# Transposes of the activation halves one group sooner, and a second group of seven products in the first down pairs

## The reference, cut to what matters

```python
h = h + (g_attn * y_attn + g_ssm * y_ssm) @ w_out[layer]
u = rms_norm(h, mlp_norm_w[layer]) @ w_up[layer]      # 2048 -> 8192
h = h + jnp.square(jax.nn.relu(u)) @ w_down[layer]    # 8192 -> 2048
```

## Time and profile before

| | |
|---|---|
| median of 3 runs | 1985.65 us (1985.53 to 1986.33) |
| profiled execution, its own time | 1987.6 us |
| its span | 1985.6 us |
| TensorE busy | 1971.4 us, 9007 matmuls |
| VectorE, ScalarE, GpSimd busy | 1487.8, 1241.7, 175.3 us |
| granted clock of TensorE, mean | 0.999 |

### The profile page before, as it was taken

One profiled execution on the slowest core, in us unless ns is written; L12 is line 12 of the kernel. 1 busy time (PEld: TensorE's weight loads), 2 busy tenths in 40 slices (PEclk: granted clock), 3 DMA queues, 4 the chain that ended last, 5 costly groups with the idle time before them and its releaser, 6 DMA issues.

```text
span 1985.6 us, 25599 instructions
## 1 busy us (share of the span) xinstructions
PE 1971.4 (99%) x9007; PEld 1628.3 (82%) x9007; DVE 1487.8 (75%) x1769; ACT 1241.7 (63%) x1427; POOL 175.3 (9%) x179
## 2 busy tenths in 40 slices
PE   9999999999999999999999999999999999999999
PEld 8888888888887888888888888888788888878877
DVE  5777777777788766677675566577798799788878
ACT  6666666767776555555774444558657755865773
POOL 2110120112232221110000000000000000000000
PEclk9999999999999999999999999999999999999999
DMA  7777887889997666666896766767767766866865
GB/s 249 207 206 201 216 205 203 216 228 247 240 225 226 198 193 192 199 191 190 224 242 193 215 200 237 212 212 217 204 220 223 207 196 207 219 209 192 233 190 170
DMA packets 332193, 419.52 MB, mean 211 GB/s; under 512 B 147248, under 2 KB 147696, under 8 KB 331840
## 3 DMA queue, kind: packets, MB, share of 16 engines
q1 hardware_dynamic: 331184, 415.23, 73.3%
q10 hardware_dynamic: 448, 2.24, 0.3%
q0 software_dynamic: 464, 0.77, 0.2%
HBM read 382.46 MB, written 2.16 MB: 194 GB/s over the span
## 4 chain that ended last, share of the span: by engine, by line
PE 85%; DVE 6%; ACT 5%; issue 2%; DMA 2%; ACTq 0%; POOL 0%; DVEq 0%; SPq 0%; POOLq 0%
PE ps L807 20%; PE ps L809 20%; PE ps L808 20%; PE ps L1104 7%; PE ps L1105 7%; PE ps L1109 7%; DVE wlo L2413 2%; ACT f_st L1777 2%; DMA f_half<-r_half 2%; ACT whi L1712 1%; DVE t_lo__92 L2424 1%; PE ps L986 1%; PE ps L755 1%; ACT ust L1740 1%; DVE wlo L2418 1%
## 5 line engine op out<-in xcount | busy, mean ns | idle before, releaser
L1848 DVE TENSOR_TENSOR wlo<-raw,whi 128x1024 fp32r<-128x1024 f32 x450 | 569.5, 1272 | 328.3 <-ACT whi L1229 326.8
L1229 ACT ACTIVATE whi<-raw 128x1024 fp32r<-128x1024 f32 x450 | 473.2, 1057 | 323.2 <-PE ps L809 312.4
L807 PE MATMUL ps<-whi,xT_hi 128*128 128x512 f32 x1268 | 498.3, 393 | 0.0
L809 PE MATMUL ps<-whi,xT_lo 128*128 128x512 f32 x1268 | 493.8, 389 | 0.0
L808 PE MATMUL ps<-wlo,xT_hi 128*128 128x512 f32 x1268 | 493.6, 389 | 0.0
L809 PEld LDWEIGHTS ps<-whi,xT_lo 128*128 128x128 f32 x1268 | 238.0, 188 | 50.2
L807 PEld LDWEIGHTS ps<-whi,xT_hi 128*128 128x128 f32 x1268 | 238.1, 188 | 48.7 <-issue 1.4
L808 PEld LDWEIGHTS ps<-wlo,xT_hi 128*128 128x128 f32 x1268 | 238.2, 188 | 47.5
L2413 DVE TENSOR_TENSOR wlo<-raw,whi 128x1024 fp32r<-128x1024 f32 x186 | 219.5, 1219 | 41.8 <-ACT whi L1712 41.8
L1712 ACT ACTIVATE whi<-raw 128x1024 fp32r<-128x1024 f32 x187 | 192.5, 1053 | 92.8 <-PE ps L1109 92.7
L1104 PE MATMUL ps<-whi,fT_hi 128*128 128x512 f32 x416 | 163.6, 393 | 6.9 <-DVE fT_lo L2521 5.8
(11 more groups left out here) (358 smaller groups left out, 2871.8 us busy)
## 6 DMA issues: line engine op xcount, KB each, us to landing
raw<-in_w_in SPq DMA_DIRECT2D x319, 512.0 KB, 4.3
raw<-in_w_up SPq DMA_DIRECT2D x128, 512.0 KB, 4.3
raw<-in_w_down SPq DMA_DIRECT2D x128, 512.0 KB, 4.6
raw<-in_w_ssm_out SPq DMA_DIRECT2D x64, 512.0 KB, 4.3
raw<-in_w_attn_out SPq DMA_DIRECT2D x32, 512.0 KB, 4.1
raw<-in_w_out SPq DMA_DIRECT2D x32, 512.0 KB, 4.2
arow<-arows SPq DMA_DIRECT2D x16, 512.0 KB, 4.9
x_in<-in_x SPq DMA_DIRECT2D x4, 512.0 KB, 8.3
```

The costliest lines, as they stand in the source:

```text
L807: mm(dst, xh, whi[sl][:, kk, :], start=(s == 0 and kk == 0), stop=False)
L809: last = mm(dst, xl, whi[sl][:, kk, :], start=False, stop=(s == US - 1 and kk == UK - 1))
L1229: A(whi[s % SLOTS][:, :, :], raw[s % SLOTS][:, :, :], ACT.Copy).then_inc(hi_ready, 1)
L1848: V.tensor_tensor(wlo[s % SLOTS][:, :, :], raw[s % SLOTS][:, :, :], fp(whi[s % SLOTS][:, :, :]), ALU.subtract).then_inc(lo_ready, 1)
```

## The change

It adds group 5 to the groups of seven in pairs 2, 6, 10 and 14 (37 in all), and places the work that belongs to it. Form 2 is summed ahead of the low weights of group 4 instead of behind them; form 1 is rounded behind group 2's turn instead of group 4's, and form 2 behind group 3's; their low parts both come behind group 3's turn; the bank sums of those pairs move from group 5 to group 6. And in all pairs that have transposes of activation halves, SP issues these behind the loads of groups 4 and 5 instead of 5 and 6.

```diff
-DOWN_SEVEN_FIRST = (0,)
+DOWN_SEVEN_FIRST = (0, 5)
...
-SUMS_AT = (6, 5, 5, 6)
+SUMS_AT = (6, 5, 6, 6)
 SUMS_LATE = ((1, 6), (2, 3))
 JOIN_FIRST = (2, 3)
-MADE_FIRST = ()
+MADE_FIRST = ((2, 3),)
 FORMS_MADE = ((1, 4), (2, 1), (2, 3))
-FORMS_HI = ((1, 5), (2, 4), (2, 5))
-FORMS_LO = ((1, 6), (2, 5), (2, 6))
+FORMS_HI = ((1, 5), (2, 2), (2, 3))
+FORMS_LO = ((1, 6), (2, 3), (2, 3))
...
-            TURN_AT = (5, 6)
+            TURN_AT = (4, 5)
```

## The result

The changed kernel takes **1989.15 us** (median of 17 runs, 1987.97 to 1990.70); the kernel before, run in turn with it on the same chip, takes 1985.52 us (17 runs, 1984.33 to 1987.67). The ratio is 1.0018, 95% interval 1.0011 to 1.0026: 3.6 us slower, where 0.3 us faster was forecast. The time lies inside the range given, on the slow side.

What follows compares the result with a forecast made beforehand. TensorE, busy for 99% of the span, was taken as the bound. Four pairs at +0.75 us, less 2.2 and 1.6, plus 0.5, gave -0.3 us: 1985.65 to 1985.3 us, range 1980.5 to 1990.3.

Steps and rivals of the forecast that it cites:

- join of the first half: Pair 2, ScalarE: joining the transposed planes begins at 1396.50 instead of 1399.06.
- wait at group 5: Pair 2, TensorE: a new wait of 1.4 us for group 5's rounded weights, where there was none.
- wait at group 6: Pair 2, TensorE: group 6 waits 0.5 us for the second half's low part.
- wait at the next pair: Behind pair 2, TensorE waits 1.3 us on the first output bank, going on at 1430.0 instead of 1429.25.
- the transposes land late: First half's transposes land 0.8 to 1.3 us late, moving the whole chain: 1988.6 to 1990.5 us; chance 0.20.
- The clock falls at the new waits: Rival: 1.4 us of waiting is enough to lower the clock, 6.4 us more: 1991.7 us; chance 0.04.
- The work is hidden after all: Rival: group 5's weights are ready at 1408.4, new waits shrink by 1.4 a pair: 1979.7 us; chance 0.20.
- The four pairs: Sum over pairs 2, 6, 10, 14: 4 x 0.75 - 2.2 - 1.6 + 0.5 = -0.3 us, carried to the median.
- The low clock's 1.6 us: Pair 10, behind its long wait at group 4: a loss of some 1.6 us that the change would remove.
- The 2.2 us: What pairs 6, 10 and 14 wait more than pair 2 goes away: 2.2 us saved.
- The +0.5: Pair 10 shows no present wait at the next pair to set off, so 0.5 us is added.
- the runs don't hold pair 10's loss: Rival: runs without a profile lack pair 10's long wait, so 3.1 us less is saved: 1988.4 us; chance 0.08.

Runs made afterwards that it cites:

- the second profile: The kernel before, unchanged, profiled again: 1985.80 us (11 runs), ratio 1.0000, profiled execution 1985.09.
- the third: The kernel before, unchanged, profiled once more: a single execution of 1985.94 us.
- the 1989.39 and 1989.67 executions: Two single profiled executions of the changed kernel, unedited, taking 1989.39 and 1989.67 us.
- the first kernel: The kernel before with only the transposes moved behind the loads of groups 4 and 5, no further group of seven: 1977.44 us, ratio 0.9956.
- the kernel with the weight sums first: The changed kernel with group 5's weight sums made ahead of the join's low part and group 4's low weights: 1988.45 us, ratio 1.0011.
- the kernel with the second group of seven alone: The changed kernel with the transposes back behind the loads of groups 5 and 6: 2001.18 us, ratio 1.0073.
- form 2 behind: The changed kernel with form 2 summed behind group 4's low weights and group 5's weight sums again: 1985.33 us, ratio 0.9998.
- the three kernels of 1977 us: The kernel before with transposes moved everywhere (1977.44 us), only in down pairs (1977.63), or everywhere with a second group of seven at group 3 (1977.82).

## Why the prediction was wrong

**The steps inside the pair were right.** The last column is worked out start to start at 0.227 us, in pair 2.

| step | forecast | measured |
|---|---|---|
| join of the first half | 1396.50 | 1396.53 |
| end of the high part | 1400.16 | 1400.18 |
| weight sums of group 5 start | 1404.54 | 1404.56 |
| weights of group 5 rounded | 1409.76 | 1409.79 |
| wait at group 5 | 1.4 | 1.38 (the others 1.50, 1.72, 1.40) |
| wait at group 6 | 0.5 | 0.35, and 0.11 behind its first matmul |
| bank sums of `h` start | some 1428.7 | 1428.79 |
| wait at the next pair | 1.3 | 1.00, and 0.27 in the matmuls around it |
| matmuls | 8995 | 8995 |

The landings came at the low end, as I had taken them: 3.0 to 3.1 us after issue in pair 2 and 3.1 to 4.4 in the other three, where 5.2 to 8.1 stood before with the loads in front. The rival "the transposes land late" is out as the cause of the 3.6 us; late landings show in one place of the four profiles, with 0.6 us. "The clock falls at the new waits" is out too: behind 1.4 to 1.7 us of waiting the granted clock stays at 1.00 in all four pairs. "The work is hidden after all" fell by the serial chain, as was said against it.

The Trainium skill, Advanced Engine Details and Errata, section X-Bar Transpose (TRN2), has transposes as fast as regular DMAs. No run here tests that: with no load shortly in front they landed after 3.0 to 4.4 us and a load of 512 KB has a median of 4.6, but a plane of 128 x 1024 two-byte elements is half of such a load. What this case shows is what the place in the queue is worth: behind two loads they took up to 8.1. The prediction bounded them by neighbouring rows and was right to.

**The step that failed is "The four pairs", and in it the transfer to the median:** 4 x 0.75 − 2.2 − 1.6 + 0.5 = −0.3, "with the same difference" taken to 1985.65. The 3.0 is there. The terms set off against it were a property of one execution:

- The low clock's 1.6 us: absent in both further profiles of the kernel before. It was also read a little small: of the nine matmuls of the earlier trace rows, eight run from start to start in 3.52 us instead of 1.82, a loss of 1.7.
- The 2.2 us that pairs 6, 10 and 14 waited more than pair 2's 1.04 each: 0.7 and 1.4 in the further two (the sums 4.8 and 5.5 less 4 x 1.04).
- The +0.5 for pair 10's missing wait at the next pair: the two further profiles have that wait in all four pairs (0.5 us each, start to start), so there is nothing to add.

Put into the same sum, the second profile gives 3.0 − 0.7 = +2.3 and the third 3.0 − 1.4 = +1.6; the medians say +3.6. In the traces, from the MLP's first matmul to its last, the changed kernel takes 686.3, 686.6, 686.8 and 687.5 us in its four profiles, and the kernel before 686.0, 683.4 and 684.3. So the first pair of profiles is 0.2 us apart there, and the first profile of the changed kernel lies 2.9 and 2.0 above the two undisturbed ones of the kernel before. That is 0.4 to 0.6 more than the sum gives, and group 5's waits in pairs 6 and 10 (1.50 and 1.72 against pair 2's 1.38) account for it. On average the four lie 3.0 us above the two in the MLP, and 3.3 us in the whole time (1988.8 and 1985.5), which is nearly the difference of the medians.

What is left is that the first profile of the changed kernel was the fastest of its 17 executions, 1.2 us under their median; the 1989.39 and 1989.67 executions hold 1.4 and 1.7 us more, in the scattered places named above. The wait at pair 12 is one of them, and it was seen only with a group of seven at group 5. Why it comes in some executions and not in others stays open.

So the rival that came true is "the runs don't hold pair 10's loss", 1988.4 us, which I gave 0.08; the measured median is 0.75 us above it. The evidence for it was on the table: the profiled execution took 1987.6 us, 1.3 above the slowest of the three runs shown (1986.33). A loss of 1.6 us in one place, seen in an execution 1.95 us above the median, is first suspected of being that difference. The prediction asked whether the runs hold it and said that this was not shown, and then carried it over as if every execution had it.

**The change itself** is two edits of opposite sign: the transposes' turn gives 8.3 us, and the second group of seven takes 11.7. By the forecast's terms it saves 2.7 us of matmuls and pays 4 x (1.4 + 0.5 + 1.3) = 12.8 us in waits, 10.1 in all, and the MLP in the two profiles is 10.2 us longer (676.1 to 686.3). The 1.5 us up to 11.7 go with the choice of executions: the profiled one of the first kernel lies 0.5 us above its median, that of the other 1.2 below. The waits come because VectorE and ScalarE have to make the forms and sums in the one stretch where both are already the last link.

## What to carry to other kernels

Before a loss read in one profile is set off in a sum, ask whether the runs hold it: if the profiled execution lies above the others by about the size of that loss, forecast from the sum without it, and let the profiled extra be the rival. Cost the two halves of an edit by themselves, because one that gains 8 us can carry one that loses 12 and still look like no change. In this kernel an operand that several products share was cheap where the engine that makes it has a pause between the last input and the due time (group 3: nothing lost), and dear in a serial stretch (group 5), where 0.94 us placed ahead of it came back as some 0.94 us, four times.

## What the hardware showed that I had not expected

- The same two transposes land 3.0 to 3.1 us after issue or 5.2 to 6.7, by what stands in the queue ahead of them (pair 2, where the first is issued at 1391.49 in both kernels). In pair 10 it was 6.8 to 8.1 us behind the two loads of 512 KB and 4.0 to 4.4 without them.
- The clock. In the first profile of the kernel before, the granted clock behind a wait of 2.36 us is 0.66 over 4 us, mostly the lower level of 1.2 GHz, and so it is in the kernel with the weight sums first, pair 10, 2.34 us idle:

```profile
1748.00:1752.00 4.00, 4.00 (x13) 3.15 (x13) 4.00 (x6) 3.97 (x5) 0.00 (x0) 0.66 0.54 177
```

  but not in that kernel's pair 14, behind a longer one:

```profile
1918.96 0.50 PE L1104 MATMUL ps<-whi,fT_hi 128*128 128x512 f32 x1 [2.48 <-DVE fT_lo L2521]
```

```profile
1919.00:1923.00 4.00, 4.00 (x17) 3.02 (x18) 3.96 (x8) 3.13 (x4) 0.00 (x0) 1.00 0.35 103
```

  In the kernel with the second group of seven alone it fell behind 1.78 us of idling in pair 10 and 2.24 in pair 14, and not behind 2.44 in pairs 2 and 6. So the length of the wait alone doesn't decide it, and it doesn't take more than 2 us of waiting, as an expectation above had it; these runs don't show what does. But the kernels with the longest waits have it most: a mean granted clock of 0.999 or less in 5 of 5 executions of that kernel, in 9 of 11 with the weight sums first, in 23 of 62 of the kernel before, in 4 of 30 of the changed kernel, in 2 of 11 with form 2 behind, and in 1 of 15 of the three kernels of 1977 us. A low stretch costs some 1.7 us each time.
